# Two directions' substitution products issued in turn, tile by tile, in a 64-row triangular solve

## The reference

```python
def wkv7_scan(r, w, k, v, kk, a, reverse):
    """S_t = S_{t-1}(diag(w_t) - kk_t^T (a_t*kk_t)) + v_t^T k_t, y_t = S_t r_t."""
    def step(state, inp):
        r_t, w_t, k_t, v_t, kk_t, a_t = inp
        sa = jnp.einsum('bhvk,bhk->bhv', state, -kk_t)
        state = (state * w_t[:, :, None, :]
                 + sa[..., :, None] * (kk_t * a_t)[..., None, :]
                 + v_t[..., :, None] * k_t[..., None, :])
        return state, jnp.einsum('bhvk,bhk->bhv', state, r_t)
...
for direction in range(2):        # forward and reverse scan, 8 heads of 64
    ys.append(wkv7_scan(..., reverse=(direction == 1)))
y = ys[0] + ys[1]
```

## Time and profile before

| | |
|---|---|
| median of 3 runs | 2052.01 us (2048.03 to 2054.74) |
| profiled execution, own time | 2049.37 us |
| its span, first to last instruction | 2047.6 us |
| mean granted TensorE clock | 0.969 of 2.4 GHz |
| PE busy | 1823.2 us, 89% of the span |
| DVE busy | 1471.7 us, 72% |
| ACT busy | 1005.7 us, 49% |
| POOL busy | 459.0 us, 22% |
| L1961 | 128 records of 213 to 267 ns, from 247.5 to 310.2 us |
| L1969 | 64 records, from 249.4 to 308.4 us |
| L1976 | 64 records, from 253.5 to 313.9 us |

### The profile page before, as it was taken

How to read it: one execution, slowest core, us unless ns; L and a number is a source line. 1 busy time by engine, 2 the same in 40 slices (tenths; PEclk the granted TensorE clock), 3 DMA queues, 4 the chain that set the end, 5 groups by cost and what they waited for, 6 DMA issues and landing times. The chain is left out here.

```text
span 2047.6 us, 34074 instructions
## 1 busy us (share of the span) xinstructions
PE 1823.2 (89%) x12602; PEld 1358.5 (66%) x12602; DVE 1471.7 (72%) x2579; ACT 1005.7 (49%) x2031; POOL 459.0 (22%) x463
## 2 busy tenths in 40 slices
PE   5978889888887878777799999889999999989998
PEld 4845887644442222222269998669998899978997
DVE  7775557887776677666476677877678887887666
ACT  3445224554544444444365554465556555556554
POOL 2010220244444444434310001002123331110000
PEclk8988999899999999999999999799999999989999
DMA  8780003799999999999955566035556556335652
GB/s 338 294 295 1 4 4 104 283 420 421 421 421 422 421 421 422 420 419 422 421 187 191 189 202 232 15 104 184 185 189 219 184 183 195 125 104 181 189 190 96
DMA packets 103123, 497.41 MB, mean 243 GB/s; under 512 B 11874, under 2 KB 16354, under 8 KB 69859
## 3 DMA queue, kind: packets, MB, share of 16 engines
q1 hardware_dynamic: 65458, 226.82, 33.2%
q0 software_dynamic: 36864, 268.45, 31.6%
q10 hardware_dynamic: 688, 0.65, 0.1%
HBM read 494.83 MB, written 1.05 MB: 242 GB/s over the span
## 5 line engine op out<-in xcount | busy, mean ns | idle before, releaser
L255 PE MATMUL ps<-srcs,wh 128*128 128x512 f32 x2000 | 706.9, 394 | 5.8 <-DVE srcs L269 1.7
L2380 PE MATMUL ps<-row,diag 128*128 128x512 f32 x1024 | 497.4, 621 | 117.1 <-ACT diag L2492 117.0
L257 PE MATMUL ps<-srcs,wl 128*128 128x256 f32 x2000 | 564.5, 282 | 0.0
L237 DVE TENSOR_TENSOR wl<-ring,wh 128x1024 fp32r<-128x1024 f32 x362 | 459.1, 1273 | 92.5 <-ACT wh L231 91.3
L2380 PEld LDWEIGHTS ps<-row,diag 128*128 128x128 f32 x1024 | 181.9, 192 | 420.4 <-ACT diag L2492 266.0
L2599 DVE CUSTOM_DVE_ANT_0 row<-row,h_tok 128x1024 f32<-128x1024 f32 x256 | 313.3, 1224 | 191.5 <-DMA row<-in_peer_uv,experts 181.4
L255 PEld LDWEIGHTS ps<-srcs,wh 128*128 128x128 f32 x2000 | 376.2, 188 | 88.1 <-issue 7.2
L231 ACT ACTIVATE wh<-ring 128x1024 fp32r<-128x1024 f32 x362 | 378.7, 1051 | 69.7 <-PE ps L257 42.0
L257 PEld LDWEIGHTS ps<-srcs,wl 128*128 128x128 f32 x2000 | 378.7, 189 | 2.5 <-issue 2.4
L2291 POOL DMA_INDIRECT row<-in_peer_uv,experts x256 | 281.0, 1098 | 383.9 <-PE ps L2380 342.1
L2485 ACT ACTIVATE acts<-dots 128x1 f32<-128x1 f32 x256 | 51.8, 202 | 329.3 <-DVE dots L2599 328.6
(11 more groups left out here) (559 smaller groups left out, 2220.6 us busy)
## 6 DMA issues: line engine op xcount, KB each, us to landing
ring<-in_stream SPq DMA_DIRECT2D x378, 512.0 KB, 3.6
alpha<-in_ada_late SPq DMA_DIRECT2D x10, 512.0 KB, 5.7
beta<-in_ada_late SPq DMA_DIRECT2D x10, 512.0 KB, 5.4
kappa<-in_ada_late SPq DMA_DIRECT2D x10, 512.0 KB, 6.0
row<-in_peer_uv,experts POOLq DMA_INDIRECT x256, 15.3
bias<-in_attn_bias SPq DMA_DIRECT2D x8, 256.0 KB, 7.7
w<-in_cmp_w SPq DMA_DIRECT2D x1, 2048.0 KB, 7.7
mats<-in_mats SPq DMA_DIRECT2D x1, 1216.0 KB, 6.6
```

Of the source, the lines that this page charges most:

```text
L237: nc.vector.tensor_tensor(wl[:, n % PAIRS, :], ring[:, tile % RING, :], wh[:, n % PAIRS, :].bitcast(F32), ALU.subtract).then_inc(tiles_fre ...
L255: nc.tensor.matmul(out, wh[:, n, cols], source.rearrange("p a t -> p (a t)"), start=start, stop=stop, skip_group_check=True)
L257: return nc.tensor.matmul(out[:, 0:S], wl[:, n, cols], source[:, 0, :], start=False, stop=stop, skip_group_check=True)
L2380: last = nc.tensor.matmul(y_part(t, half), diag[:, s % DIAGS, :], row[:, s % ROWS, D + half * 512:D + (half + 1) * 512], start=(slot == 0) ...
```

## The change

Each group now holds both directions. The 16 products of a step alternate between d = 0 and d = 1, head by head, and ahead of the first one stand the waits of both directions. The last product of each direction still raises its own semaphore.

```diff
-                    for b, turn in ((0, 0), (1, 1)):
+                    for turn in range(2):
                         for d in range(2):
-                            r, other = half_rows(d ^ b), half_rows(1 - (d ^ b))
                             if turn == 0:
                                 pe.wait_ge(xt_ready[d], len(LEVELS) + 1)
                                 pe.wait_ge(early_ready[d], 1)
                             else:
                                 pe.wait_ge(late_ready[d], 1)
-                            for at in range(NH):
-                                last = nc.tensor.matmul(ps[r, Y_BANK[d], at * HALF:(at + 1) * HALF], XT[d][other, at, :],
-                                                        G[d][other, at, :], start=True, stop=True)
-                            last.then_inc(u_done[d], 1)
+                        for at in range(NH):
+                            last = []
+                            for d in range(2):
+                                r, other = half_rows(d ^ turn), half_rows(1 - (d ^ turn))
+                                last.append(nc.tensor.matmul(ps[r, Y_BANK[d], at * HALF:(at + 1) * HALF], XT[d][other, at, :],
+                                                             G[d][other, at, :], start=True, stop=True))
+                        for d in range(2):
+                            last[d].then_inc(u_done[d], 1)
                         if turn == 0:
                             for d in range(2):
-                                early = half_rows(d)
                                 pe.wait_ge(sa_ready[d], 1)
-                                for at in range(NH):
-                                    last = nc.tensor.matmul(ps[early, G_BANK[d], at * HALF:(at + 1) * HALF],
-                                                            cross[early, at, :], SA[d][early, at, :], start=False,
-                                                            stop=True, skip_group_check=True)
-                                last.then_inc(late_done[d], 1)
+                            for at in range(NH):
+                                last = []
+                                for d in range(2):
+                                    early = half_rows(d)
+                                    last.append(nc.tensor.matmul(ps[early, G_BANK[d], at * HALF:(at + 1) * HALF],
+                                                                 cross[early, at, :], SA[d][early, at, :], start=False,
+                                                                 stop=True, skip_group_check=True))
+                            for d in range(2):
+                                last[d].then_inc(late_done[d], 1)
```

## The result

The changed kernel takes 2069.27 us (median of 6, 2065.56 to 2077.6) against 2053.3 us of before (6 runs, 2048.03 to 2057.46). The ratio is 1.0076, with a 95% interval of 1.0057 to 1.0096: slower by about 15.6 us. The forecast was 4.5 us slower.

The account below looks back on a forecast made before the run. PE, always busy in two 6.00 us substitutions, was taken to hide each direction's copies; exposing them adds 2.24 us per solve, 4.5 in all: 2052.0 + 4.5 = 2056.5 us, range 2054 to 2059, whole range 2050 to 2061.5.

Parts of the forecast that it names:

- PE's time: Substitution: rival that PE's halved time counts and copies stay hidden, 5.6 us faster in all, 2046.4 us; 3 in 100.
- a double group: Substitution products: 32 records on two tiles take as long as a single group, 1.19 us to the reader.
- the pair of negations: Substitution, after the first u group: both directions' DVE negations lie on the path, 1.41 us.
- of ACT copies: Substitution, after the cross group: both directions' copies on ACT lie on the path, 1.21 us.
- nothing behind takes up a delay: Behind both substitutions: a delay passes through in full; the rival that something absorbs it, 2052.0 us, had 5 in 100.
- 2.24 us in each solve: Both substitutions: the way to the y products grows from 4.82 to 7.06 us, 4.5 us in all.
- The hand-overs: Substitution: from the end of a copy to the first PE record that waited for it, taken as 0.06 us.
- The clock falls: Substitutions: rival that PE's pauses lower its clock, 3.4 us on top of 4.5, 2059.9 us; 20 in 100.
- from 264 to 268 PE was busy for 2.34 of 4 us: Window of the kernel before with a 1.65 us pause and clock at 1.00, cited against the clock falling.
- the pause of 3 us: PE's 3.04 us standstill before 201.68 in the kernel before, after which the clock fell; compared with three short pauses.
- Work of 3.4 us at half speed loses 1.7 us: Price of a clock fall in one substitution: 1.7 us, at most perhaps double.
- the length of one chain alone: Substitution: one direction's products, copies and hand-overs without a second copy take 5.72 us, against 4.82 before.

Follow-up runs that it names:

- fillers: Changed kernel plus one unread 128x512 product behind the first double u group and one behind the double cross group; 1.0018 of the kernel before.
- u paired: Kernel before with only the u products alternating between directions behind double waits, cross products as before; 1.0062 of the kernel before.
- half the products: Kernel before with only the first four heads' u and cross products made, order and waits unchanged; 1.0016 of the kernel before.
- split copies: Changed kernel with ACT taking the negations of d = 1 and DVE its cross copy; 1.0049 of the kernel before.
- waits only: Kernel before, its product order kept, with both directions' waits put ahead of each pair of groups; 1.0099 of the kernel before.
- u products twice: Changed kernel with every u product issued twice in a row; 1.0058 of the kernel before.
- a filler at 201 us: Kernel before with three unread 128x512 products where PE stands still from 198.6 to 201.7 us; 0.9993 of the kernel before.

## Why the prediction was wrong

**Right:** that PE's time was not what the change could win; that a double group takes as long as a single one (1.18 and 1.19 us to its reader, forecast 1.19); the pair of negations (1.41, forecast 1.41) and of ACT copies (1.21); and that nothing behind takes up a delay. The rule of the Trainium skill ("TensorEngine Tiling (Array Packing)", section Theoretical Speedup) held for the products alone, 1.04 us of weight loads in place of 1.76, and said nothing of the kernel's time, as argued.

**A term too small:** "**2.24 us in each solve**" measured 2.49, 2.54 (with fillers) and 2.48 (without). The hand-overs, taken as 0.06, are 0.11 for the groups that wait for both directions (251.70 + 1.41 = 253.11, PE at 253.22), and 0.23 for the group with four waits (XT[1] ready at 250.29, PE at 250.52). The y products, with one wait, still start 0.06 after theirs though PE stood still for 0.75 us before them (257.73 + 0.69 = 258.42, PE at 258.48), as did the cross group in the run with u paired (0.05). So the longer hand-over goes with the number of waits and not with the pause.

**The step that failed:** under "The clock falls", the weight given to "from 264 to 268 PE was busy for 2.34 of 4 us ... and the clock stayed at 1.00". I took one sparse window without a fall as evidence that three pauses would pass, and gave the fall 20 in 100. It came in both substitutions of both profiles, from 254.7 for 13.7 us and from 319.5 for 17.1 us in the first. And the window was luck: behind the very same pause the clock fell in seven of thirteen profiles, the changed kernel's both among them. The run with half the products shows the fall without a pause above 0.5 us; so the pause of 3 us, with which I compared, was the wrong measure.

**And its price:** "Work of 3.4 us at half speed loses 1.7 us" took the length of the lower stretch from the transposes near 202, which were followed by a barrier. Here it lasted 13.7 and 17.1 us, since the y and state products that came next did not bring the clock back. In the two substitutions together it cost 7.4 - 5.0 = 2.4 us in W and 7.9 in T, 10.3 in all; the rival's figure was 3.4. By the times, the changed kernel with fillers stands 0.58% below the one without, 12 us. So the rival named the right mechanism, at a third of its price.

Shown by experiment: the waits' 5.0 us, the clock's 10 to 12, that fillers undo the second and not the first, and that a fall needs no double wait. Only argued: which property of PE's work the clock follows. The runs say that busy time alone is not it, and that the same work can have either outcome (the second solve's pause).

## What to carry to other kernels

Two independent chains that stand half a step apart hide each other's copies; issuing them together to pack the array halves the time of the products and puts both copies and every hand-over on the path. First ask whether products or copies set the pace: the length of one chain alone (here 5.7 us by the estimate of the prediction) is the floor for the packed form, which took 6.1 us at its best (split copies, W2).

Before a gap is put into PE's stream, look at what runs behind it. Here the y and state products took most of the cost of the lower clock: the price of the fall was set by the 13.7 and 17.1 us that it lasted, and not by the pause of 1.3 us in which it began. Where a gap can't be avoided, one unread full-size product in it is worth a trial: here two in each substitution gave back 10 us by the profiles and 12 of 16 by the times. And a clock that held behind a pause in one profile is no evidence that it holds: look at several. The Trainium skill ("TensorE: Matmul & The Clock Gate", section "Loop structure matters more than you think") says that the loop nest decides whether products stay at the full clock and asks for them back to back; the runs agree in that the same y products ran at 1.00 behind the order of before and at 0.50 behind the changed one.

## What was not expected of the hardware

- y and state products (128x64, 16 records to a group for y) did not end the lower level: in the changed kernel they ran at 0.50 for 10 us with PE busy for 4.00 of 4 us, where they had run at 1.00 in the kernel before. Behind two 128x512 products, 3.6 us at 0.50, the full clock was back within 0.4 us, in both substitutions.
- The clock fell although PE had been busy for 1.87 of 3 us on single 64x64 tiles (waits only), stayed up with PE busy for 1.44 of 4 us on two (u products twice), and fell 1 us (half the products) and 2.5 us (u products twice) into the y products.
- One and the same pause in the second solve, 1.6 to 1.9 us long, was followed by a fall within 1.5 us in seven profiles and by none in six; the kernel before and the same with a filler at 201 us, with 1.65 us each, stand on either side.
- Eight float32 64x64 products on each of two tiles take as long as eight on one tile: 1.18 and 1.19 us from first record to reader against 1.18, with two banks as with one.
